# Second-phase shift and scale of both mLSTM layers as dot products on VectorE in the q and k stage, tiles laid out by output channel

## The chip, the cores and the metric

The kernel runs on one core of a Trainium2 chip. The metric is the device time of one execution in microseconds; lower is better. Times of whole executions are given as the median of several runs, and one further execution was recorded by the hardware profiler.

## What is computed

The reference is one inference step of a four-layer trunk for two groups of 128 tokens (context and latent) with width 1024. Layers 0 and 3 mix tokens with an mLSTM, layer 1 with windowed attention, layer 2 with neighbourhood attention. Around every mixer and every ConvFFN stands a norm whose shift, scale and gate are linear in SiLU of a condition vector:

```python
sc = jax.nn.silu(c_ctx)
sl = jax.nn.silu(c)
for i in range(DEPTH):
    mod_c = (sc @ ada_w[i] + ada_b[i]).reshape(6, D_MODEL)
    mod_l = (sl @ ada_w[i] + ada_b[i]).reshape(Bd, 6, 1, D_MODEL)
    hc = _rmsnorm(xc, norm_w[i, 0]) * (1.0 + mod_c[1]) + mod_c[0]
    ...                                   # token mixer: oc, ol
    xc = xc + mod_c[2] * oc
    hc = _rmsnorm(xc, norm_w[i, 1]) * (1.0 + mod_c[4]) + mod_c[3]
    xc = xc + mod_c[5] * _conv_ffn(hc, ...)
```

`ada_w[i]` is 1024 x 6144 in float32. The change concerns `mod[3]` and `mod[4]` (shift and scale ahead of the ConvFFN) of layers 0 and 3: 2048 columns of `ada_w[i]` for each of the two condition vectors.

## The kernel before, in words

All weights come as one stream of tiles, 128 partitions x 2048 float32 (1 MB each), in an order that `stream_order` fixes. SyncE's queue loads them into a ring of four buffers, `raw[0..3]` (L515 to L528). Tile n may be loaded once the tile four places ahead of it in the stream has been released; the loop issues strictly in stream order, so a tile whose buffer is not free also holds back all tiles behind it. 374 tiles go by.

A weight tile is split in two halves of 1024 columns. For each half ScalarE writes a rounded high part (`split_hi`, L460) and VectorE the rest (`split_lo`, L471), into rings of four halves, `spl_hi` and `spl_lo`; TensorE multiplies with both parts. VectorE's `lo_done` releases the raw buffer; TensorE's `half_used` releases the slot of the halves.

An `ada` tile is not split. It has 128 input channels as partitions and 2048 outputs (two of the six vectors) as columns. `ada(i, g)` (L677) multiplies it directly as float32 into the bank `ADA_PS`, in four strips that run beside each other; 8 tiles make a phase, 3 phases a layer, 96 tiles in all. When a phase is complete, `copy_mod` (VectorE, L1676) adds the bias, `mod_rows` (TensorE, L693) transposes, and `mod_columns` (VectorE, L1686) copies into `coef_g` (phase 1, gates) or `coef_b` and `coef_a` (phases 0 and 2, shift and scale; for the scale there follow +1 and the norm's weight). `fill(count)` puts ada tiles between other work; the tables `NORM_FILL`, `CONV_FILL`, `HEAD_FILL`, `V_FILL`, `FFN_FILL` say how many go where.

Each engine's program is written out by hand, in the order in which it runs, with semaphores between engines. An mLSTM layer has these stages:

- ml_x: 8 tiles, convolution, SiLU; then `CONV_FILL` ada tiles and the gates' product.
- q and k: 16 tiles, `ml_qk`, in 8 groups g of two tiles; the first four groups make Q, the last four K. In group g TensorE takes tiles 2g and 2g+1 (`queries_keys`, L569 and L571). VectorE's list for the group is `split_lo` of tile 2g+1, in groups 1 and 2 of Q some small row operations (absolute value, scans, L1845 to L1878), `split_lo` of tile 2g+2, and `with_low` (L1835), which adds the low half of the product to what ScalarE copied out of PSUM. `with_low` must wait until TensorE has finished tile 2g+1. Tile 16 is the first of the v stage.
- scores and transposes (L779, L785), then v: 16 tiles.
- heads: for each of four heads `values`, `state`, `HEAD_FILL` ada tiles, one z tile (`gate_z`, L554 to L556), `head_rows` (L902, transposes of what VectorE normalised in `head`), and another z tile. In layer 0 the gates' `mod_rows` stands behind head 0, in layer 3 in the q and k stage; that of phase 2 stands in head 3 in both.
- down projection, 8 tiles, residual, norm, ConvFFN.

## Time and profile before

| | |
|---|---|
| median of three runs | 1875.69 us (1871.1 to 1875.8) |
| profiled execution, its own time | 1871.99 us |
| span in the profile | 1870.1 us |
| TensorE (PE) busy | 1812.6 us, 97% |
| TensorE weight loads (PEld) | 1501.6 us, 80% |
| VectorE (DVE) busy | 1341.8 us, 72% |
| ScalarE (ACT) busy | 981.0 us, 52% |
| GpSimd (POOL) busy | 178.6 us, 10% |
| DMA | 418.12 MB, mean 224 GB/s |

Busy time is a share of the span. The chain of waits follows the work that ended last back from the last instruction. In rows of the timeline the first number is the start, the second the duration of the row's instructions together, both in us; in brackets stands how long the engine had been idle ahead of it and what released it. "L471" is line 471 of the kernel.

### The profile page before, as it was taken

The numbers are of one execution on the slowest core, as the hardware profiler recorded it, in microseconds if no ns is written. First come the engines' busy times: TensorE is split into PE (matmuls) and PEld (weight loads), VectorE is DVE, ScalarE is ACT, GpSimd is POOL, SyncE is SP. The second block draws the span as 40 slices with busy tenths as digits, with TensorE's granted clock in tenths as the row PEclk, the third lists the DMA queues.
The fourth block names the chain that finished last, engine by engine and source line by source line (L and its number), as shares of the span: only waits on it lengthen the run. The fifth ranks groups of instructions, "written<-read, shape, count | busy, mean of one in ns | idle before, by whom it ended". The sixth has DMA issues, their size and how long they took to land.

```text
span 1870.1 us, 27382 instructions
## 1 busy us (share of the span) xinstructions
PE 1812.6 (97%) x11100; PEld 1501.6 (80%) x11100; DVE 1341.8 (72%) x1973; ACT 981.0 (52%) x1470; POOL 178.6 (10%) x154
## 2 busy tenths in 40 slices
PE   5999999999999999999999999999999999999998
PEld 2988777797888767888877778888888786878888
DVE  3864677668897566998656688966765776769984
ACT  2754445545674354766344466745643445447653
POOL 2100121001000113000011210002100210020001
PEclk8999999999999999999999999999999999999999
DMA  9565556867655757665574766556555647645542
GB/s 365 190 231 195 199 201 229 316 231 275 247 183 198 267 207 292 246 240 189 194 299 172 295 268 267 180 195 242 223 191 184 229 173 286 232 168 195 193 171 84
DMA packets 72527, 418.12 MB, mean 224 GB/s; under 512 B 12176, under 2 KB 18696, under 8 KB 24144
## 3 DMA queue, kind: packets, MB, share of 16 engines
q1 hardware_dynamic: 54288, 392.98, 56.1%
q10 hardware_dynamic: 18112, 23.38, 3.9%
q8 instruction: 88, 1.44, 0.3%
q14 instruction: 39, 0.32, 0.0%
HBM read 405.35 MB, written 10.95 MB: 223 GB/s over the span
## 4 chain that ended last, share of the span: by engine, by line
PE 87%; DVE 5%; DMA 2%; ACT 2%; issue 2%; POOL 1%; POOLq 0%; SPq 0%; DVEq 0%; ACTq 0%
PE ps L587 18%; PE ps L605 9%; PE ps L637 9%; PE ps L589 9%; PE ps L569 6%; PE ps L621 5%; PE ps L638 4%; PE ps L571 3%; PE ps L677 3%; PE ps L554 3%; PE ps L555 3%; PE ps L556 3%; DMA raw<-in_stream 2%; DVE spl_lo L471 2%; PE ps L884 1%
## 5 line engine op out<-in xcount | busy, mean ns | idle before, releaser
L471 DVE TENSOR_TENSOR spl_lo<-raw,spl_hi 128x1024 fp32r<-128x1024 f32 x556 | 686.8, 1258 | 191.3 <-ACT spl_hi L460 191.0
L460 ACT ACTIVATE spl_hi<-raw 128x1024 fp32r<-128x1024 f32 x556 | 574.0, 1053 | 302.6 <-PE ps L638 112.0
L587 PE MATMUL ps<-H,spl_hi 128*128 128x512 f32 x1408 | 496.5, 398 | 4.0 <-DVE H L1750 4.0
L589 PE MATMUL ps<-H,spl_lo 128*128 128x256 f32 x1408 | 393.3, 279 | 0.0
L587 PEld LDWEIGHTS ps<-H,spl_hi 128*128 128x128 f32 x1408 | 264.3, 188 | 79.1 <-issue 15.7
L589 PEld LDWEIGHTS ps<-H,spl_lo 128*128 128x128 f32 x1408 | 265.4, 188 | 0.0
L637 PE MATMUL ps<-G,spl_hi 128*128 128x512 f32 x528 | 184.1, 395 | 0.0
L569 PE MATMUL ps<-B,spl_hi 128*128 128x512 f32 x512 | 179.8, 397 | 0.0
L554 PE MATMUL ps<-H,spl_hi 128*128 128x256 f32 x512 | 148.0, 289 | 6.3 <-DVE H L1750 4.7
L638 PE MATMUL ps<-G,spl_lo 128*128 128x256 f32 x528 | 146.8, 278 | 0.0
L555 PE MATMUL ps<-H,spl_hi 128*128 128x256 f32 x512 | 146.0, 285 | 0.0
L556 PE MATMUL ps<-H,spl_lo 128*128 128x256 f32 x512 | 145.9, 285 | 0.0
L571 PE MATMUL ps<-B,spl_lo 128*128 128x256 f32 x512 | 143.1, 279 | 0.0
L605 PE MATMUL ps<-spl_hi,A 128*128 128x512 f32 x512 | 140.0, 391 | 2.6 <-DVE knat L1888 1.7
L677 PE MATMUL ps<-raw,cond_wide 128*32 128x512 f32 x768 | 103.3, 638 | 20.9 <-DMA raw<-in_stream 11.3
L637 PEld LDWEIGHTS ps<-G,spl_hi 128*128 128x128 f32 x528 | 99.1, 188 | 23.4
L569 PEld LDWEIGHTS ps<-B,spl_hi 128*128 128x128 f32 x512 | 96.1, 188 | 23.3
L605 PEld LDWEIGHTS ps<-spl_hi,A 128*128 128x128 f32 x512 | 95.2, 188 | 23.9 <-ACT v L1187 2.6
L1187 ACT ACTIVATE up<-ps 128x512 f32<-128x512 f32 x88 | 52.6, 598 | 116.3 <-PE ps L589 116.3
L554 PEld LDWEIGHTS ps<-H,spl_hi 128*128 128x128 f32 x512 | 99.2, 194 | 16.1 <-issue 16.0
L555 PEld LDWEIGHTS ps<-H,spl_hi 128*128 128x128 f32 x512 | 99.3, 194 | 0.1
L556 PEld LDWEIGHTS ps<-H,spl_lo 128*128 128x128 f32 x512 | 99.3, 194 | 0.0
(248 smaller groups left out, 2963.4 us busy)
## 6 DMA issues: line engine op xcount, KB each, us to landing
raw<-in_stream SPq DMA_DIRECT2D x374, 1024.0 KB, 4.9
out_new_C<-c_stage ACTq DMA_DIRECT2D x16, 512.0 KB, 3.9
ada_b<-in_ada_b ACTq DMA_DIRECT2D x4, 768.0 KB, 9.9
E<-rows_out ACTq DMA_DIRECT2D x8, 256.0 KB, 4.3
Em<-rows_out ACTq DMA_DIRECT2D x8, 256.0 KB, 4.6
x<-in_x ACTq DMA_DIRECT2D x1, 1024.0 KB, 11.9
wide<-rows_out ACTq DMA_DIRECT2D x8, 128.0 KB, 4.7
cache<-in_na_cache ACTq DMA_DIRECT2D x1, 1024.0 KB, 9.0
```

The lines of the kernel that those rows point to most:

```text
L460: act.activation(spl_hi[m % SPL][:, :], raw[r % RAW][:, h * HALF:(h + 1) * HALF], ACT.Copy).then_inc(S["hi_done"], 1)
L471: dve.tensor_tensor(spl_lo[m % SPL][:, :], raw[r % RAW][:, h * HALF:(h + 1) * HALF], spl_hi[m % SPL][:, :].bitcast(F32), ALU.subtract).the ...
L554: pe.matmul(out, w_hi, x_hi, start=st, stop=False, skip_group_check=True)
L555: pe.matmul(out, w_hi, x_lo, start=False, stop=False, skip_group_check=True)
L556: mm = pe.matmul(out, w_lo, x_hi, start=False, stop=en, skip_group_check=True)
L569: pe.matmul(v3(banks[b][:, :], TOK), w_hi, B_both[:, kk], start=kk == 0, stop=False, skip_group_check=True)
L571: mm = pe.matmul(banks[b][:, 0:TOK], w_lo, B_both[:, kk, 0], start=False, stop=kk == KI - 1, skip_group_check=True)
L587: pe.matmul(banks[:, b * 512:(b + 1) * 512], w_hi, H[:, kk * 512:(kk + 1) * 512], start=kk == 0, stop=False, skip_group_check=True)
L589: mm = pe.matmul(banks[:, b * 512:b * 512 + TOK], w_lo, H[:, kk * 512:kk * 512 + TOK], start=False, stop=kk == KD - 1, skip_group_check=True)
L605: mm = pe.matmul(ACC[2 * s + c][:, :], a, w[m % SPL][:, c * 512:(c + 1) * 512], start=st, stop=en, skip_group_check=True)
L637: pe.matmul(v3(bank[:, :], TOK) if nk == KI else bank[:, :], w_hi, rows(k), start=k == 0, stop=False, skip_group_check=True)
L638: mm = pe.matmul(bank[:, 0:TOK], w_lo, chunk(k)[0], start=False, stop=k == nk - 1, skip_group_check=True)
```

## The change

Of layers 0 and 3 the 8 tiles of phase 2 are no longer `ada` tiles but `ada_column` tiles: same weights, same size, transposed. A tile holds 128 output channels as partitions; its columns 0 to 1023 are the 1024 input channels of the shift, 1024 to 2047 those of the scale. The silu'd condition vectors stand on every partition (`cond_all`, 2048 columns), and each sum over 1024 inputs is one VectorE instruction that multiplies elementwise, writes the products into PSUM (`two[2]`, not read) and the sum into a column of `dots`. Four of them belong to a tile, two in `dot(g, 0)` and two in `dot(g, 1)`; each waits for the one ahead.

The tiles enter the stream in the q and k stage, one in each group, ahead of tiles 2g+2 and 2g+3. `ada` tiles leave the heads (10 and 7 become 2 and 0) and the conv stage of layer 3 (3 becomes 2). The condition vectors are silu'd once at the start as rows, written to DRAM, and read back onto all partitions in each mLSTM layer. `RB` and `RBW` move to a place of their own, since `cond_all` takes theirs. In layer 3 `mod_rows` of the gates moves from the q and k stage to behind head 0. At the end of the heads two additions of the bias and the scale's step make `coef_b` and `coef_a` from `dots`.

```diff
-CONV_FILL = {0: 3, 3: 3}
+CONV_FILL = {0: 3, 3: 2}
 V_FILL = 1
-HEAD_FILL = {0: [2, 3, 3, 2], 3: [2, 2, 2, 1]}
+HEAD_FILL = {0: [2, 0, 0, 0], 3: [0, 0, 0, 0]}
+COLUMN_LAYERS = [0, 3]
...
             order.append(qk[0])
             fill(CONV_FILL[i])
-            order += qk[1:]
+            order.append(qk[1])
+            for g in range(8):
+                order += [("ada_column", i, g)] + qk[2 * g + 2:2 * g + 4]
...
                 if last[0] == "ada":
                     sp.wait_ge(S["ada_used"], INDEX[last] + 1)
+                elif last[0] == "ada_column":
+                    sp.wait_ge(S["dot_done"], 4 * INDEX[last] + 4)
                 else:
                     sp.wait_ge(S["lo_done"], 2 * INDEX[last] + 2)
...
                     queries_keys(n0 + t, 8 * (t % 2), ACC[t // 2 % 2 * 2:t // 2 % 2 * 2 + 2])
-                    if t == 3 and i:
-                        mod_rows(i, 1)
...
-                    if h == 0 and i == 0:
+                    if h == 0:
                         mod_rows(i, 1)
-                    if h + 1 == MH:
-                        mod_rows(i, 2)
...
                     if g == 0:
+                        act.wait_ge(S["condr_kept"], 16)
+                        act.wait_ge(S["xc_lo"], 2 + 8 * (j + 1))
+                        act.wait_ge(S["xcs_done"], 2 + 8 * (j + 1))
+                        act.dma_start(cond_all[:, :], cond_out.rearrange("a b -> (a b)").unsqueeze(0)
+                                      .to_broadcast([P, NS * D])).then_inc(S["conda_landed"], 16)
...
+                act.wait_ge(S["dot_done"], 32 * (j + 1))
                 state_rows(j, 0)
...
+            act.dma_start(cond_row[:, :], io["cond_rows"]).then_inc(S["condr_landed"], 16)
+            act.wait_ge(S["condr_landed"], 16)
+            act.activation(cond_row[:, :], cond_row[:, :], ACT.Silu).then_inc(S["condr_silu"], 1)
+            act.wait_ge(S["condr_silu"], 1)
+            act.dma_start(cond_out, cond_row[:, :]).then_inc(S["condr_kept"], 16)
...
+                def dot(g, n):
+
+                    tile = ("ada_column", i, g)
+                    r = POS[tile]
+                    if n == 0:
+                        landed(dve, r)
+                        if g == 0:
+                            dve.wait_ge(S["conda_landed"], 16 * (j + 1))
+                    for s in range(NS):
+                        o = (n * KD + g) * NS + s
+                        if g + n + s:
+                            dve.wait_ge(S["dot_done"], 32 * j + 4 * g + 2 * n + s)
+                        dve.scalar_tensor_tensor(two[2][:, :], raw[r % RAW][:, n * D:(n + 1) * D], 1.0,
+                                                 cond_all[:, s * D:(s + 1) * D], ALU.mult, ALU.mult,
+                                                 accum_out=dots[:, o:o + 1]).then_inc(S["dot_done"], 1)
...
                     split_lo(dve, n0 + 2 * g + 2)
+                    dot(g, 0)
                     with_low(Q, g, g, DK ** -0.5)
+                    dot(g, 1)
                 for g in range(4):
                     splits(n0 + 8 + 2 * g, 2)
+                    dot(4 + g, 0)
+                    if g == 3:
+                        dot(4 + g, 1)
                     with_low(K, g, 4 + g, 1.0)
+                    if g < 3:
+                        dot(4 + g, 1)
...
-                mod_columns(i, 2)
+                link.wait()
+                dve.wait_ge(S["dot_done"], 32 * (j + 1))
+                for n, coef in enumerate((coef_b, coef_a)):
+                    o = (2 * j + n) * KD
+                    link(dve.tensor_tensor(v3(coef[:, :], NS), v3(dots[:, n * KD * NS:(n + 1) * KD * NS], NS),
+                                           sc("ada_c", o, KD).unsqueeze(2).to_broadcast([P, KD, NS]), ALU.add))
```

## Rows read from the trace of the kernel before

**Rows 1.** The page: busy time by engine, and the chain that ended last.
```profile
PE 1812.6 (97%) x11100; PEld 1501.6 (80%) x11100; DVE 1341.8 (72%) x1973; ACT 981.0 (52%) x1470; POOL 178.6 (10%) x154
...
PE 87%; DVE 5%; DMA 2%; ACT 2%; issue 2%; POOL 1%; POOLq 0%; SPq 0%; DVEq 0%; ACTq 0%
```

**Rows 2.** PE's waits, longest of all: total, times, longest, in us.
```profile
PE ps L677 <- DMA raw<-in_stream: 11.3, 10, 2.4
```

**Rows 3.** Windows: length; busy PE, PEld, DVE, ACT, POOL; clock, DMA share, GB/s.
```profile
38.00:45.00 7.00, 3.75 (x20) 3.50 (x17) 6.79 (x7) 1.64 (x3) 3.88 (x3) 0.68 0.57 209
...
102.00:192.00 90.00, 88.74 (x503) 76.70 (x502) 47.05 (x62) 40.27 (x52) 0.00 (x0) 1.00 0.54 198
301.00:388.00 87.00, 87.00 (x560) 65.00 (x559) 57.53 (x84) 42.77 (x62) 3.54 (x8) 1.00 0.83 309
```

**Rows 4.** Timeline of DVE, one group of the q and k stage, layer 0.
```profile
145.77 0.76 DVE L1835 SCALAR_TENSOR_TENSOR Q<-ps,Q 128x256 f32<-128x256 f32 x2 [3.76 <-ACT Q L1187]
146.99 3.56 DVE L471 TENSOR_TENSOR spl_lo<-raw,spl_hi 128x1024 fp32r<-128x1024 f32 x3 [0.47 <-ACT spl_hi L460]
152.10 1.23 DVE L471 TENSOR_TENSOR spl_lo<-raw,spl_hi 128x1024 fp32r<-128x1024 f32 x1 [1.55 <-ACT spl_hi L460]
157.07 0.76 DVE L1835 SCALAR_TENSOR_TENSOR K<-ps,K 128x256 f32<-128x256 f32 x2 [3.75 <-ACT K L1187]
```

**Rows 5.** Timeline of ACT in the same group.
```profile
148.23 1.06 ACT L460 ACTIVATE spl_hi<-raw 128x1024 fp32r<-128x1024 f32 x1 [0.33 <-PE ps L571]
```

**Rows 6.** Line L528, tiles issued from 100 to 192 us: time to landing.
```profile
DMA to landing us min/median/max: 4.6/4.7/7.3
```

**Rows 7.** Line L528, two tiles issued 0.4 us apart.
```profile
L528 SPq DMA_DIRECT2D raw<-in_stream x2: 328/380/431, 92.6 to 93.0; - x2
...
DMA to landing us min/median/max: 4.8/5.9/7.0
```

**Rows 8.** Timeline of DVE, q and k stage of layer 0.
```profile
111.85 0.75 DVE L1835 SCALAR_TENSOR_TENSOR Q<-ps,Q 128x256 f32<-128x256 f32 x2 [3.76 <-ACT Q L1187]
...
126.65 0.41 DVE L1850 TENSOR_TENSOR gM<-gM,gA 36x256 f32<-36x256 f32 x1
...
130.92 0.41 DVE L1872 SCALAR_TENSOR_TENSOR RB<-gb,gG 36x256 f32<-36x256 f32 x1
131.36 0.32 DVE L1878 TENSOR_SCALAR m_out<-RB 4x1 f32<-4x1 f32 x2
...
190.99 0.75 DVE L1835 SCALAR_TENSOR_TENSOR K<-ps,K 128x256 f32<-128x256 f32 x2 [3.75 <-ACT K L1187]
```

**Rows 9.** The same timeline, layer 3: first and last `with_low`.
```profile
1350.35 0.76 DVE L1835 SCALAR_TENSOR_TENSOR Q<-ps,Q 128x256 f32<-128x256 f32 x2 [3.76 <-ACT Q L1187]
...
1428.66 0.75 DVE L1835 SCALAR_TENSOR_TENSOR K<-ps,K 128x256 f32<-128x256 f32 x2 [3.65 <-ACT K L1187]
```

**Rows 10.** Timeline of ACT, layer 1: exponentials that also sum.
```profile
688.45 0.19 ACT L1475 ACTIVATION_READ_ACCUMULATOR Ea<-ps,nm 128x1 f32 x1
688.54 0.47 ACT L1475 ACTIVATE Ea<-ps,nm 128x256 f32<-128x256 f32 x1
```

**Rows 11.** Timeline of DVE, layer 1: a small operation and one that waits for it.
```profile
687.88 0.16 DVE L2085 SCALAR_TENSOR_TENSOR nm<-mx,nsink 128x4 f32<-128x4 f32 x1
688.08 0.16 DVE L2088 TENSOR_TENSOR esink<-nm,nsink 128x4 f32<-128x4 f32 x1
```

**Rows 12.** Chain of waits: last ada tile ahead of the first norm; heads of layer 0.
```profile
24.80 1.06 PE ps L677 x8
...
324.72 2.71 PE ps L677 x24
...
371.41 1.85 PE ps L677 x16
```

**Rows 13.** Timeline of DVE, layer 3, head 3.
```profile
1611.09 0.69 DVE L1676 TENSOR_TENSOR mod_b<-ps,ada_b 128x512 f32<-128x512 f32 x1
```

**Rows 14.** Timeline of ACT at the start.
```profile
13.10 1.15 ACT L1204 ACTIVATE sq<-x 128x512 f32<-128x512 f32 x2 [3.96 <-DMA x<-in_x]
```

More of the change, by code:

```diff
@@ L83, in stream_order @@
     order = []
-    adas = iter([("ada", i, g) for i in range(DEPTH) for g in range(ADA_TILES)])
+    adas = iter([("ada", i, g) for i in range(DEPTH)
+                 for g in range(2 * ADA_PHASE if i in COLUMN_LAYERS else ADA_TILES)])
     def fill(count):
@@ L150, with mod_index @@
 ADAS = [tile for tile in ORDER if tile[0] == "ada"]
-MAIN = [tile for tile in ORDER if tile[0] != "ada"]
-INDEX = {tile: n for tiles in (MAIN, ADAS) for n, tile in enumerate(tiles)}
+COLUMNS = [tile for tile in ORDER if tile[0] == "ada_column"]
+MAIN = [tile for tile in ORDER if tile[0] not in ("ada", "ada_column")]
+INDEX = {tile: n for tiles in (MAIN, ADAS, COLUMNS) for n, tile in enumerate(tiles)}
+def mod_index(i, phase):
+    return 3 * i + phase - sum(l < i for l in COLUMN_LAYERS)
 def chunked(w, k0, nk, c0, nc):
@@ L191, in host_tile @@
         return np.concatenate([rows[:, v * D:(v + 1) * D] for v in MOD_SOURCE[2 * p:2 * p + 2]], 1)
+    if kind == "ada_column":
+        o = P * tile[2]
+        return np.concatenate([w["ada_w"][i][:, v * D + o:v * D + o + P].T for v in MOD_SOURCE[4:6]], 1)
     if kind == "ml_x":
@@ L266, in host_arrays @@
     put("cond", np.stack([columns(w["c_ctx"]), columns(w["c"][0])], 2).reshape(P, 2 * KD))
+    put("ada_c", np.concatenate([columns(w["ada_b"][i].reshape(6, D)[v]) for i in COLUMN_LAYERS
+                                 for v in MOD_SOURCE[4:6]], 1))
     ada_b = np.zeros((DEPTH, 4, 32, 3, ADA_N), f)
@@ L339, in build @@
     ow = [sb(f"ow{b}", 2 * TOK, F32, rW + 4 * KB + 2 * KB * b) for b in range(2)]
-    RB = sb("RB", 2 * TOK, F32, rW)
-    RBW = sb("RBW", T, F32, rW + 2 * KB)
+    cond_all = sb("cond_all", NS * D, F32, rW)
+    cond_out = nc.dram_tensor("cond_out", (16, P), F32, kind="Internal").ap()
     wide = [sb(f"wide{b}", 2 * T, F32, rW + 4 * KB + KB * b) for b in range(2)]
@@ L388, in build @@
     ccol = small_sb("ccol", NS * 36)
+    RB, RBW = small_sb("RB", 2 * TOK), small_sb("RBW", T)
+    dots = small_sb("dots", 2 * KD * NS)
+    cond_row = small_sb("cond_row", P, rows=16)
     gI, gF, gA, gM, gb, gc, gG = (small_sb(n, TOK) for n in ("gI", "gF", "gA", "gM", "gb", "gc", "gG"))
@@ L672, in ada @@
                 r = POS["ada", i, g]
-                if k == 0 and 3 * i + phase:
-                    pe.wait_ge(S["modT_done"], 3 * i + phase)
+                if k == 0 and i + phase:
+                    pe.wait_ge(S["modT_done"], mod_index(i, phase))
                 landed(pe, r)
@@ L689, in mod_rows @@
             def mod_rows(i, phase):
-                pe.wait_ge(S["modb_done"], 3 * i + phase + 1)
+                pe.wait_ge(S["modb_done"], mod_index(i, phase) + 1)
                 for b in range(4):
@@ L1651, in _ @@
                 if i + 1 < DEPTH:
-                    act.wait_ge(S["modb_done"], 3 * i + 3)
+                    act.wait_ge(S["modb_done"], mod_index(i + 1, 0))
                     act.dma_start(ada_b[:, :], io["ada_b"][i + 1]).then_inc(S["adab_landed"], 16)
@@ L1679, in mod_columns @@
             def mod_columns(i, phase):
-                dve.wait_ge(S["modT_mm"], 3 * i + phase + 1)
+                dve.wait_ge(S["modT_mm"], mod_index(i, phase) + 1)
                 if phase != 1 and link.n:
@@ L1688, in mod_columns @@
                 if phase != 1:
-                    dve.wait_ge(S["modT_done"], 3 * i + phase + 1)
+                    dve.wait_ge(S["modT_done"], mod_index(i, phase) + 1)
                     nw = sc("norm_w", (2 * i + phase // 2) * KD, KD)
@@ L1840, in mlstm @@
                     split_lo(dve, n0 + 2 * g + 1)
-                    if g == 2 and i:
-                        mod_columns(i, 1)
                     if g == 1:
@@ L1931, in mlstm @@
                 split_c(1)
-                if i == 0:
-                    copy_mod(i, 1)
+                copy_mod(i, 1)
                 head_columns(j, 0)
@@ L1939, in mlstm @@
                 z_lo(1)
-                if i == 0:
-                    mod_columns(i, 1)
+                mod_columns(i, 1)
                 for h in range(1, MH):
@@ L1946, in mlstm @@
                     split_z(2 * h + 1)
-                    if h + 1 == MH:
-                        copy_mod(i, 2)
                     head_columns(j, h)
@@ L1959, in mlstm @@
                         split_z(2 * h + 2)
-                mod_columns(i, 2)
+                link.wait()
[4 more added lines that the diff above has]
+                                           sc("ada_c", o, KD).unsqueeze(2).to_broadcast([P, KD, NS]), ALU.add))
+                link.wait()
+                link(dve.scalar_tensor_tensor(v3(coef_a[:, :], NS), v3(coef_a[:, :], NS), 1.0,
+                                              sc("norm_w", (2 * i + 1) * KD, KD).unsqueeze(2).to_broadcast([P, KD, NS]),
+                                              ALU.add, ALU.mult))
                 project(INDEX["ml_down", i, 0], 8, KI, 2 * i)
```

7 lines of the change are left out of this document (3 added, 4 removed).

## The prediction, made before the changed kernel was run

> **What bounds the kernel now.** I read the page first: PE is busy for 97% of the span and holds 87% of the chain that ended last; DVE is busy for 72% [rows 1]. PE's waits come next: the longest in total, ada tiles waiting for their weights, is 11.3 us in the whole span [rows 2]. So the kernel is bound by PE's work, and taking matmuls away should pay if nothing else falls late. The windows say where there is room: in the q and k stage DVE is busy 47 of 90 us, in the heads 57.5 of 87, with PE full in both [rows 3]. By busy shares the change looks good: it moves work from the full engine to a half-empty one. What decides, though, is when the new work stands in DVE's list and when it frees a buffer, so the timeline of one q and k group came next, and the landing times of the tiles behind it.
>
> **One group before.** A group lasts from 145.77 to 157.07, 11.3 us [rows 4]; all of it is PE's two tiles of 5.65 us. DVE adds the low half (0.76), splits three halves (3.56) and, when ACT has it ready, a fourth (1.23), then idles 3.75 us until PE is done. ACT's first high half of a tile takes 1.06 and waits for a slot that PE frees, not for a landing [rows 5]: a tile is asked for four tiles ahead, and lands in 4.7 us [rows 6].
>
> **What is added, step by step.** First one dot. Its operands are 1024 float32, as in `split_lo`; of three of these behind each other two cost (3.56 - 1.23)/2 = 1.17 each [rows 4]. A sum that is written out was seen on ACT only: a read of the accumulator of 0.19 follows the main operation, and the next main one starts 0.09 after the read does [rows 10]. A small DVE operation takes 0.16, and one that waits for it starts 0.20 after its start [rows 11]. The dots wait for each other, so I take 1.17 + 0.20 = 1.37 us from start to start. Bounds: 1.17 if sum and wait are free; 1.5 if the read starts only once the main one has ended and PSUM as a target adds its share. A tile has four: 5.5 us, 44 a layer. The Trainium skill (VectorE: DVE Perf Modes, Two Vector instructions with no wait between them) also counts an operation that writes out its accumulator as two instructions; the trace shows this on ACT alone, and by it the sum would lie near my value and not at the low bound.
>
> By load alone this fits: 0.76 + 4.8 (two tiles' splits) + 5.5 = 11.0 of 11.3 us. But look at the ring. In the stream a group is column tile g, then weight tiles 2g+2 and 2g+3. Four places behind column tile g stands weight tile 2g+4, so SyncE asks for it only when the last of the four dots of g is done, and everything behind it in the stream waits as well. DVE's list from there: end of `dot(g, 1)`; split of tile 2g+3 (2.4 us, in the buffer already); split of tile 2g+4; `dot(g+1, 0)`; `with_low`; `dot(g+1, 1)`. The second split must wait for the landing, and all that is behind it in DVE's list waits too, the dots that free the next buffer among them. So this is a closed cycle:
>
> - landing of a tile: 4.7 median in this stage [rows 6]; a second one is issued right behind it, but of two tiles 0.4 us apart the first landed in 4.8 and only the second in 7.0 [rows 7]. With the semaphore 4.85;
> - high half by ACT, 1.06 [rows 5], and 0.03 until DVE starts: 1.09;
> - two low halves, 1.17 + 1.23 less the overlap: 2.36;
> - two dots, 2.73; `with_low`, 0.76; two dots, 2.73. `with_low` finds PE done: tile 2g+3 starts when its first half is split, 1.2 us into the cycle, and ends at 6.9.
>
> Sum 14.5 us against 11.3, and PE idles for the difference, in two gaps (before 2g+3, its half came late; before 2g+4). Which of the ends of the unknown costs I take hardly matters for the sign: with dots of 1.17 and a landing of 4.6 the cycle is 13.6, still 2.3 above PE's need. It would be PE's again only with dots of 0.55.
>
> The first groups, in layer 0: `with_low` of group 0 starts at 111.85 as before [rows 8]; two dots end at 115.3. Group 1: split of tile 3 until 117.7, row operations 0.6, tile 4 lands at 120.2, its low halves are done at 123.65, dots, `with_low`, dots: 129.9. Group 2: split of tile 5 until 132.25; then the scans, from 126.65 to 131.68 before, 5.05 us [rows 8], which stand ahead of the second split and cover the landing here: 137.3; split 2.36, dots and `with_low` 6.2: 145.9. Groups 3 to 6: 4 x 14.5 = 58. Group 7 has all dots ahead of `with_low`; its end is that of one more cycle: 218.4. Before, the last `with_low` ended at 190.99 + 0.75 = 191.74 [rows 8]. **Layer 0: +26.7 us.** Layer 3 runs the same list; from its first `with_low` to the end of the last it took 1429.41 - 1350.35 = 79.06 before [rows 9] and takes 218.4 - 111.85 = 106.55: **+27.5 us.** The scores and the v stage behind it wait for `with_low` of group 7 and shift whole; the v tiles' buffers are free by then.
>
> **What is removed.** An ada tile in a run costs PE 2.71 / 3 = 0.90 to 1.85 / 2 = 0.93 [rows 12]. Layer 0's heads lose 3, 3 and 2: 7.3 us, and the transposes of phase 2, 0.35. The z tiles that stood behind the fills were split some 2.7 us or more ahead there, so PE takes the whole of it. Layer 3 loses one tile in the conv stage (0.9), 2 in each of heads 0 to 2 and 1 in head 3. There the gates' `mod_rows` now stands behind head 0 and waits for DVE, whose list is not earlier; I count 2.2 for heads 0 and 1 together, 1.85 for head 2 and 1.45 for head 3, where before PE waited for `mod_b` at 1611.09 [rows 13] and now waits for the z tile split just ahead of it. Layer 3: 6.4. **Removed: 14.1 us.** Its bounds: 16 x 0.92 = 14.7 if no cover is missing, 9 if layer 3's heads hang on DVE throughout.
>
> Edits with no price: at the start ACT now waits for `cond_row` to land, behind `x` and `ada_b` in its queue, before the squares, which began at 13.10 [rows 14]. I expect them near 19, done near 24.5; PE adds them up only after the ada tile of 24.80 [rows 12], so 1.4 us of cover is left, and what exceeds it costs as much. `cond_all`, 1 MB, is asked for at about 99 and is first needed at 108; if it lands up to 3 us late, DVE's idle time ahead of 111.85 takes it. The moved `RB`, the bias as columns, the final additions: nothing. GpSimd does nothing in this stage [rows 3].
>
> **Sum.** 1870.1 + 26.7 + 27.5 - 14.1 = 1910.2 us of span, 1912.1 as the profiled execution's own time (1871.99 before, so 1.9 around the span). The median of the runs before is 3.7 above that execution, though its lowest run is 0.9 below it; I add half and say **1914 us**, 2% slower. Bounds: dots of 1.17 or 1.5 give -13 or +8 over two layers, landings of 4.6 give -1, fills -0.6 to +5. If the first tile too suffers from the one issued behind it (7.0 instead of 4.8, in 12 cycles), +26.
>
> **The rivals.**
>
> *The cycle does not close, DVE keeps up* (faster or equal). This needs tile 2g+4 to be there when DVE comes to it. For it: DVE idles 3.75 + 1.55 us in a group, 5.3, nearly the dots' time, and halves are split up to four ahead. Against it: the release hangs on the fourth dot. Only the scans and ACT's extra functions in groups 1 and 2 would then cost, 3 to 6 us a layer. 1870.1 - 14.1 + 9 + 3.7 = 1869 us; it decides if a group of the changed kernel stays below 11.4 us.
>
> *Dots at half rate*: the sum makes each element take twice as long. Another 1.17 for each dot, the pace of 1024 elements [rows 4], is 4.7 in a group; 8 groups and two layers give +75, about 1989 us. DVE alone would then need 15.7 of 11.3 us, so no ring is needed for a loss. Against it stands that a scalar_tensor_tensor on two SBUF sources takes 0.41 on 256 columns, no more than a tensor_tensor [rows 8]; but neither writes a sum. The Trainium skill (Vector Engine (DVE) Microarchitecture Reference, Points that are easy to get wrong) states this rule for two sources that are not bf16: no read port is left for the accumulator. The trace disagrees where there is no sum, and shows no case with one.
>
> *The clock falls.* In the gaps of the cycle PE might be granted 1.2 GHz instead of 2.4, as in the stretch from 38 to 45 us, where the mean was 0.68 after thin work at the start [rows 3]. Each such stretch of 7 us costs at most 3.5 us of PE's work, and as much is idle in a cycle, so even this gives +0 to +20: 1914 to 1934. PE stays 78% busy here; I think it unlikely.
>
> *The change does not do what it says*: tiles or dots elsewhere than in this stage. Nothing in the code speaks for it.
>
> **How the numbers follow.** The closed cycle as summed, 1893 to 1925: 0.70. The cycle with slower landings or a lower clock, up to 1945: 0.11. Half rate, 1970 to 2000: 0.08. DVE keeps up, 1862 to 1875: 0.08, most of it faster by more than 0.3%, which is about what a measurement of this kernel can tell from no change. Small losses between 1875 and 1893: 0.03. The range that holds 8 in 10 is 1893 to 1945; faster 0.06, same 0.03, slower 0.91.
>
> **What would show it.** In the timeline of DVE in the k groups, one `with_low` every 14.5 us; ahead of every second split a wait for ACT's `spl_hi`, and ACT there released by the landing instead of by PE; PE with waits for `spl_lo` of some 3 us a group, about 45 to 50 us in all where now there are next to none; tile 2g+4 issued within 0.1 us of the fourth dot's end; dots of 1.2 with a read of the accumulator behind each of about 0.16. The heads of layer 0 should be 7.7 us shorter. I am wrong if the group stays at 11.3, if the tile is issued ahead of the dots' end, or if a dot takes over 2 us.

## The result, and the profile after

The changed kernel takes 1912.4 us (median of 5 runs, 1909.0 to 1913.9) against 1875.7 for the kernel before (5 runs, 1870.2 to 1876.4). The ratio is 1.0218, with an interval of 1.0200 to 1.0235: 2.2% slower. The forecast was 1914. The profiled execution took 1912.8 us with a span of 1911.0; that of before had 1870.1, so the two traces are compared over +40.9 us.

The page of the changed kernel, busy times and chain, to be held against [rows 1]:

```profile
PE 1820.4 (95%) x10964; PEld 1512.3 (79%) x10964; DVE 1416.4 (74%) x2099; ACT 980.7 (51%) x1471; POOL 178.5 (9%) x154
...
PE 77%; DVE 11%; DMA 5%; ACT 2%; issue 2%; POOL 2%; ACTq 0%; POOLq 0%; SPq 0%; DVEq 0%
```

136 matmuls fewer were recorded, DVE has 75 us more, and it still has a quarter of the span free. What has changed is the chain: PE's part falls from 87% to 77%, DVE's and the landings' part rises from 7% to 16%. PE's waits at two lines stand out (total, times, longest, in us). Before, the first did not show at all, and the second, at L779 there, was 2.5 in total:

```profile
PE ps L590 <- DVE spl_lo L490: 23.3, 18, 2.0
PE ps L798 <- DVE K L1877: 14.3, 2, 7.3
```

L590 is the q and k projection, L798 the scores behind it. Both stand at the stage that received the dots. Windows of that stage (length; busy PE, PEld, DVE, ACT, POOL; clock, DMA share, GB/s) and of the stretch between layer 0's heads and layer 3's q and k stage, to be held against [rows 3]:

```profile
102.00:192.00 90.00, 80.68 (x433) 68.46 (x432) 67.02 (x101) 33.09 (x43) 0.00 (x0) 0.96 0.58 230
...
403.74:1372.83 969.09, 951.01 (x6022) 787.14 (x6021) 729.23 (x1142) 537.37 (x843) 94.33 (x72) 0.99 0.62 232
```

DVE is busy 67 of 90 us where it was 47, PE only 80.7 where it was 88.7. Neither engine is full, which points to a round that goes through both and through something else. DVE's timeline shows it, one group of the k half in layer 0 (start, duration, and in brackets the idle time ahead of the row with its releaser), to be held against [rows 4]:

```profile
170.52 0.75 DVE L1877 SCALAR_TENSOR_TENSOR K<-ps,K 128x256 f32<-128x256 f32 x2
171.19 1.22 DVE L1869 SCALAR_TENSOR_TENSOR ps<-raw,cond_all 128x1024 f32<-128x1024 f32 x1
172.33 0.14 DVE L1869 DVE_READ_ACCUMULATOR ps<-raw,cond_all 128x1 f32 x1
172.50 1.23 DVE L1869 SCALAR_TENSOR_TENSOR ps<-raw,cond_all 128x1024 f32<-128x1024 f32 x1
173.66 0.14 DVE L1869 DVE_READ_ACCUMULATOR ps<-raw,cond_all 128x1 f32 x1
173.66 2.35 DVE L490 TENSOR_TENSOR spl_lo<-raw,spl_hi 128x1024 fp32r<-128x1024 f32 x2
179.75 2.36 DVE L490 TENSOR_TENSOR spl_lo<-raw,spl_hi 128x1024 fp32r<-128x1024 f32 x2 [3.75 <-ACT spl_hi L479]
182.03 1.23 DVE L1869 SCALAR_TENSOR_TENSOR ps<-raw,cond_all 128x1024 f32<-128x1024 f32 x1
...
184.50 0.75 DVE L1877 SCALAR_TENSOR_TENSOR K<-ps,K 128x256 f32<-128x256 f32 x2
```

SyncE's queue and ACT in the same group:

```profile
173.82 2.54 SPq L549 DMA_DIRECT2D raw<-in_stream  x3
...
178.66 2.01 ACT L479 ACTIVATE spl_hi<-raw 128x1024 fp32r<-128x1024 f32 x2 [8.22 <-DMA raw<-in_stream]
```

Read it as one round. The fourth dot's sum is out at 173.80. SyncE issues the next loads at 173.82. DVE splits the two halves of the tile that is already there and then stands still for 3.75 us. ACT, idle for 8.22 us, is released by the landing at 178.66, DVE by ACT at 179.75, and only then come the next dots, which free the next buffer. `with_low` comes at 170.52 and 184.50: 13.98 us for a group, where before it was 11.3 [rows 4]. The idle time of DVE is about the same length as before (3.75), but then it waited for PE at the end of a group, and PE was full; now it waits for memory while PE has run dry.

The first and last `with_low` of both layers, to be held against [rows 8, 9]:

```profile
113.55 0.76 DVE L1877 SCALAR_TENSOR_TENSOR Q<-ps,Q 128x256 f32<-128x256 f32 x2 [1.23 <-ACT Q L1204]
...
215.21 0.42 DVE L1877 SCALAR_TENSOR_TENSOR K<-ps,K 128x256 f32<-128x256 f32 x1
...
1372.83 0.43 DVE L1877 SCALAR_TENSOR_TENSOR Q<-ps,Q 128x256 f32<-128x256 f32 x1 [1.12 <-ACT Q L1204]
...
1474.47 0.75 DVE L1877 SCALAR_TENSOR_TENSOR K<-ps,K 128x256 f32<-128x256 f32 x2
```

From these and the same marks before, the 40.9 us are laid out as follows (us; the stage runs from the first `with_low` to the end of the last; "heads" run from the first product of head 0's `values` to the first of the down projection):

| stretch | before | after | difference | forecast |
|---|---|---|---|---|
| start to first `with_low`, layer 0 | 111.85 | 113.55 | +1.7 | 0 |
| q and k stage, layer 0 | 79.9 | 102.4 | +22.5 | +26.7 |
| scores and v stage, layer 0 | 107.7 | 109.4 | +1.7 | 0 |
| heads, layer 0 | 86.7 | 78.4 | -8.3 | -7.65 |
| to layer 3's first `with_low` | 964.2 | 969.1 | +4.9 | -0.9 |
| q and k stage, layer 3 | 79.1 | 102.4 | +23.3 | +27.5 |
| scores and v stage, layer 3 | 107.7 | 109.5 | +1.8 | 0 |
| heads, layer 3 | 81.0 | 73.7 | -7.3 | -5.5 |
| the rest | | | +0.6 | 0 |
| sum | | | +40.9 | +40.1 |

That the total was met within 2 us is in part luck, because several misses cancel: the stages lost 8.4 us less than forecast, the heads gave 2.5 us more, and some 11 us were lost in places where the forecast has nothing.

### The profile page after: what moved, and what is told of

Its sections match the earlier page's. It is cut to its first block, busy times and chain, and to the rows that moved or that the text cites. A ratio compares the mean times of both kernels' runs of the same rounds, so it can differ in the third digit from the quotient of the medians.

```text
span 1911.0 us, 27255 instructions
## 1 busy us (share of the span) xinstructions
PE 1820.4 (95%) x10964; PEld 1512.3 (79%) x10964; DVE 1416.4 (74%) x2099; ACT 980.7 (51%) x1471; POOL 178.5 (9%) x154
## 4 chain that ended last, share of the span: by engine, by line
PE 77%; DVE 11%; DMA 5%; ACT 2%; issue 2%; POOL 2%; ACTq 0%; POOLq 0%; SPq 0%; DVEq 0%
PE ps L608 17%; PE ps L626 9%; PE ps L658 9%; PE ps L610 9%; DMA raw<-in_stream 5%; PE ps L659 4%; PE ps L642 4%; DVE ps L1869 4%; DVE spl_lo L490 3%; PE ps L575 3%; PE ps L576 3%; PE ps L577 2%; PE ps L698 2%; PE ps L901 1%; PE ps L669 1%
## 5 line engine op out<-in xcount | busy, mean ns | idle before, releaser
L608 PEld LDWEIGHTS ps<-H,spl_hi 128*128 128x128 f32 x1408 | 265.1, 188 | 78.7 <-issue 14.5
L610 PEld LDWEIGHTS ps<-H,spl_lo 128*128 128x128 f32 x1408 | 266.6, 189 | 0.0
L590 PE MATMUL ps<-B,spl_hi 128*128 128x512 f32 x512 | 188.3, 409 | 23.3 <-DVE spl_lo L490 23.3
L590 PEld LDWEIGHTS ps<-B,spl_hi 128*128 128x128 f32 x512 | 99.1, 194 | 52.4 <-DVE spl_lo L490 23.2
L698 PE MATMUL ps<-raw,cond_wide 128*32 128x512 f32 x640 | 90.1, 662 | 18.3 <-ACT cond_wide L1204 9.1
L659 PEld LDWEIGHTS ps<-G,spl_lo 128*128 128x128 f32 x528 | 99.7, 189 | 0.0
```

The costliest lines, as they stand in the source:

```text
L590: pe.matmul(v3(banks[b][:, :], TOK), w_hi, B_both[:, kk], start=kk == 0, stop=False, skip_group_check=True)
L608: pe.matmul(banks[:, b * 512:(b + 1) * 512], w_hi, H[:, kk * 512:(kk + 1) * 512], start=kk == 0, stop=False, skip_group_check=True)
L610: mm = pe.matmul(banks[:, b * 512:b * 512 + TOK], w_lo, H[:, kk * 512:kk * 512 + TOK], start=False, stop=kk == KD - 1, skip_group_check=True)
L659: mm = pe.matmul(bank[:, 0:TOK], w_lo, chunk(k)[0], start=False, stop=k == nk - 1, skip_group_check=True)
```

## The experiments

Two theories stood against each other for the 45.8 us of the q and k stages. *Ring*: the release of a buffer hangs on the fourth dot, and landing, split and dots form a closed round. *Load*: DVE simply has more to do than fits, and every dot costs its time. They part where the work is kept and only the place of the column tile in the stream is changed. The first four kernels ran on one chip beside 9 runs of before (1870.4 us), `e5` and `e6` beside 7 (1870.6), the last two beside 19 (1870.5).

**The column tile one place later.** The work of every engine is as in the changed kernel; weight tile 2g+4 now stands two places behind column tile g, and four behind weight tile 2g+1, which is split early.

```diff
-                order += [("ada_column", i, g)] + qk[2 * g + 2:2 * g + 4]
+                order += qk[2 * g + 2:2 * g + 3] + [("ada_column", i, g)] + qk[2 * g + 3:2 * g + 4]
```

> The same instructions as in the changed kernel; only the column tile moves one place back in the stream, from ahead of tile 2g+2 to between 2g+2 and 2g+3. Its buffer then goes to tile 2g+5 and not to 2g+4, which VectorE needs a whole group later. Ring theory: the waits of 3.7 us ahead of every second split vanish, a group falls from 13.95 to about 11.3 us, and q and k from the first with_low to the end of the last take 80.5 (102.4 less the six waits) to 85 us; the median 1865 to 1876, about 1869. Load theory (VectorE has too much in its list, wherever the tiles come from): the groups stay at 13 to 14 us, over 1900.

Measured: 1878.7 us (1876.1 to 1882.4), ratio 1.0051 [1.0033, 1.0068]. One line of order takes the loss from 2.2% to 0.5%: some 31 us, three quarters of it. In layer 0's stage one wait for a landing is left, 1.2 us of ACT; its length is 88.7 us (113.23 to 201.96) instead of 102.4. The ring is shown, load is refuted as the main cause. But both lie above what I had expected (1865 to 1876 us, a stage of 80.5 to 85): 8.8 us remained in layer 0 and 7.4 in layer 3 (86.5 for 79.1), so part of "load" was right after all. `with_low` of the k groups in DVE's timeline:

```profile
165.79 0.76 DVE L1877 SCALAR_TENSOR_TENSOR K<-ps,K 128x256 f32<-128x256 f32 x2 [1.02 <-ACT K L1204]
...
177.10 0.76 DVE L1877 SCALAR_TENSOR_TENSOR K<-ps,K 128x256 f32<-128x256 f32 x2 [1.02 <-ACT K L1204]
...
188.40 0.76 DVE L1877 SCALAR_TENSOR_TENSOR K<-ps,K 128x256 f32<-128x256 f32 x2 [1.00 <-ACT K L1204]
...
201.21 0.75 DVE L1877 SCALAR_TENSOR_TENSOR K<-ps,K 128x256 f32<-128x256 f32 x2
```

A group takes 11.31, as before, and DVE now waits 1.0 for ACT's copy of PE's product in it instead of 3.75. The last one takes 12.8: there all four dots stand ahead of `with_low`. The rest was lost in groups 1 to 3, the first of it here:

```profile
122.22 2.36 DVE L490 TENSOR_TENSOR spl_lo<-raw,spl_hi 128x1024 fp32r<-128x1024 f32 x2 [2.96 <-ACT spl_hi L479]
...
119.09 0.42 ACT L1302 ACTIVATE gA<-gA 36x256 f32<-36x256 f32 x1 [2.42 <-DVE gA L1885]
119.52 1.28 ACT L1304 ACT_TABLE_LOAD   x1
120.82 0.42 ACT L1304 ACTIVATE gA<-gA 36x256 f32<-36x256 f32 x1
121.14 2.00 ACT L479 ACTIVATE spl_hi<-raw 128x1024 fp32r<-128x1024 f32 x2
```

DVE waits for ACT's high half. ACT had it in its list behind an exponential and a logarithm, and these had waited 2.42 us for a row operation which DVE reached only behind its dots and a split: a round of two engines in each other's way, with no DMA in it. The wait itself is not new: before, DVE waited the same 2.96 us at this place (its split at 118.92) and then another 1.86 ahead of `with_low`. With the dots in its list there is no such slack behind it.

**All four dots ahead of `with_low`**, stream as in the changed kernel.

```diff
                     dot(g, 0)
-                    with_low(Q, g, g, DK ** -0.5)
                     dot(g, 1)
+                    with_low(Q, g, g, DK ** -0.5)
```

(and likewise for k.)

> All four dots ahead of with_low in every group; the instructions and the stream are those of the changed kernel. Ring theory: with_low (0.68) moves into the time of the landing, so a cycle is 13.95 - 0.68 = 13.3 us and some 12 cycles give -8: about 1904. Load theory: nothing changes, 1912. A theory by which with_low, and so TensorE, sets the pace would make it slower.

Measured: 1900.8 us (1899.6 to 1905.4), ratio 1.0168 [1.0147, 1.0188], against 1.0218 for the changed kernel: 0.5%, some 9 us. Two neighbouring groups in DVE's timeline:

```profile
157.46 0.75 DVE L1877 SCALAR_TENSOR_TENSOR Q<-ps,Q 128x256 f32<-128x256 f32 x2
...
163.47 2.36 DVE L490 TENSOR_TENSOR spl_lo<-raw,spl_hi 128x1024 fp32r<-128x1024 f32 x2 [2.99 <-ACT spl_hi L479]
...
170.86 0.75 DVE L1877 SCALAR_TENSOR_TENSOR K<-ps,K 128x256 f32<-128x256 f32 x2
```

The group is 13.40 instead of 13.98: the 0.67 us of `with_low` have left the way from landing to release and lie in the wait (2.99 instead of 3.75). Work on a closed round counts for its full length, the same work beside it for nothing.

**Dots half as wide**, everything else as changed.

```diff
-dve.scalar_tensor_tensor(two[2][:, :], raw[r % RAW][:, n * D:(n + 1) * D], 1.0, cond_all[:, s * D:(s + 1) * D], ...
+dve.scalar_tensor_tensor(two[2][:, 0:512], raw[r % RAW][:, n * D:n * D + 512], 1.0, cond_all[:, s * D:s * D + 512], ...
```

> Each dot goes over 512 of its 1024 columns (the sums are left half done). A dot falls by 0.53 us to 0.79. Ring theory: a cycle of 13.95 - 4 x 0.53 = 11.8 us, still 0.5 above TensorE's need, with a shorter wait for the landing in no group: the waits ahead of the second splits stay at 3.7 us. Load theory: VectorE is far below its limit, groups at 11.3, no such waits. One execution about 1878 (ring) or about 1870 (load).

Measured: 1878.5 us in a single run, so the time alone says little; the trace says more. One round in DVE's timeline:

```profile
169.54 2.36 DVE L490 TENSOR_TENSOR spl_lo<-raw,spl_hi 128x1024 fp32r<-128x1024 f32 x2 [3.67 <-ACT spl_hi L479]
171.82 0.69 DVE L1869 SCALAR_TENSOR_TENSOR ps<-raw,cond_all 128x512 f32<-128x512 f32 x1
172.60 0.70 DVE L1869 SCALAR_TENSOR_TENSOR ps<-raw,cond_all 128x512 f32<-128x512 f32 x1
173.22 0.75 DVE L1877 SCALAR_TENSOR_TENSOR K<-ps,K 128x256 f32<-128x256 f32 x2
...
181.37 2.36 DVE L490 TENSOR_TENSOR spl_lo<-raw,spl_hi 128x1024 fp32r<-128x1024 f32 x2 [3.73 <-ACT spl_hi L479]
```

The round falls to 11.83 (169.54 to 181.37), by 4 x (1.32 - 0.79) = 2.1, and DVE's wait for the landing does not change at all: shorter dots were not used to wait longer, as they would be if another engine set the pace. A round that shrinks by exactly what is taken off it is closed.

**The removal alone.** The kernel before, with the 16 fill tiles of phase 2 taken out of the heads and the conv stage and nothing put in.

```diff
-HEAD_FILL = {0: [2, 3, 3, 2], 3: [2, 2, 2, 1]}
+HEAD_FILL = {0: [2, 0, 0, 0], 3: [0, 0, 0, 0]}
...
-    adas = iter([("ada", i, g) for i in range(DEPTH) for g in range(ADA_TILES)])
+    adas = iter([("ada", i, g) for i in range(DEPTH)
+                 for g in range(2 * ADA_PHASE if i in COLUMN_LAYERS else ADA_TILES)])
```

> The kernel before with the removed part alone: the 16 phase-2 tiles of layers 0 and 3 and what follows from them are left out (the second norms of these layers use the first norms' shift and scale), mod_rows of layer 3's gates stands behind head 0. This prices what the change takes away. By the traces: heads -7.9 and -7.3, conv stage of layer 3 nothing: 1875.7 - 15 = 1861. By the sum of the prediction -14.1: 1861.6. If the fills only covered waits: above 1870.

Measured: 1854.9 us (1853.7 to 1855.5), ratio 0.9916 [0.9896, 0.9935], so 15.5 us below before; the expected 1861 had started from a higher time of before (1875.7). That is what the change had to win if the dots cost nothing. Its first `with_low` stood at 111.83, as before (111.85). From the last `with_low` of layer 0 to the first of layer 3 it takes 1152.6 us, 6.8 less than before; in this stretch the heads of layer 0 lost their eight fill tiles and the conv stage of layer 3 one:

```profile
190.96 0.76 DVE L1835 SCALAR_TENSOR_TENSOR K<-ps,K 128x256 f32<-128x256 f32 x2 [3.74 <-ACT K L1190]
...
1343.55 0.76 DVE L1835 SCALAR_TENSOR_TENSOR Q<-ps,Q 128x256 f32<-128x256 f32 x2 [3.76 <-ACT Q L1190]
```

Not all of the 15.5 us need be the removal's. The two traces differ by 16.4 us, and 3.2 of them lie behind the heads of layer 3 (248.9 us to the end for 252.0), in the last ConvFFN, where no instruction has changed; the kernel with all dots ahead of `with_low` shows 248.9 there too. Up to there the removal won 13.3 us: 7.9 and 7.3 in the heads, less 1.1 in the middle and 0.8 in layer 3's q and k stage.

**Can the win be had?** With up to 15.5 us to win, and 8.8 and 7.4 left in the two stages by the later column tile, DVE's own order was next: dots ahead of `with_low` where it waits, the row operations ahead of the split that ACT's list blocks, and the last group's dots out of the way of its `with_low`. This kernel and the three behind it keep the stream of the first experiment.

```diff
                     dot(g, 0)
-                    with_low(Q, g, g, DK ** -0.5)
                     dot(g, 1)
+                    with_low(Q, g, g, DK ** -0.5)
+                    if g == 0:
+                        (the two row operations gA, gM, moved here from group 1)
...
-                    dot(4 + g, 0)
-                    if g == 3:
-                        dot(4 + g, 1)
+                    if g < 3:
+                        dot(4 + g, 0)
+                        dot(4 + g, 1)
                     with_low(K, g, 4 + g, 1.0)
-                    if g < 3:
-                        dot(4 + g, 1)
+                dot(7, 0)
+                dot(7, 1)
```

> The kernel of e1_one_later with three moves in VectorE's own program. In the groups 0 to 6 both pairs of dots stand ahead of the evacuation with the low parts; in group 7 both stand behind it; and the two row operations that ScalarE's exponential and logarithm wait for stand at the end of group 0 instead of behind the first split of group 1. Theory: what e1_one_later still costs (8.8 us a layer in the q and k stage) is idle time of VectorE that comes from the order of its own program: 2.96 us in group 1 (ScalarE's split parts behind its logarithm), 2.00 in group 3 and 1.02 in each K group ahead of with_low (waiting for ScalarE's copy), and 5.3 of dots ahead of the last with_low. In a K group VectorE's work is 11.31 - 1.02 = 10.3 us, the before kernel's cycle is 10.0. So the stretch from with_low(0) to the last with_low falls from 88.7 to 80.5 to 84 us, K groups come 10.2 to 10.5 us apart, 2 to 5 us of the gain are given back where the dots of group 7 run ahead of the copies of ST: 1862 to 1872 us. Rival: VectorE is simply full in this stage, and each dot costs its time wherever it stands: the stretch stays at 87 to 89 us, the time within 3 us of e1_one_later's 1878.7.

Measured: 1878.1 us (1877.0 to 1881.5), ratio 1.0042 [1.0027, 1.0057]. The stage did what was expected of it: its first and last `with_low` stand at 113.74 and 193.48, 79.7 us apart, against 79.1 before. In layer 0 the dots now cost next to nothing there; in layer 3 the stage still takes 82.3 for 79.1. And the kernel is no faster: 1878.1 is the time that the rival named, though not for its reason, since the stage does not stay at 87 to 89. The place where the gain went is behind the stage (SyncE's queue, ACT's queue, DVE, in that order, then PE's wait):

```profile
199.44 0.80 SPq L549 DMA_DIRECT2D raw<-in_stream  x2
...
204.62 0.33 SPq L549 DMA_DIRECT2D raw<-in_stream  x1
...
199.52 0.41 ACTq L1409 DMA_DIRECT2D E<-rows_out  x1
199.96 0.49 ACTq L1409 DMA_DIRECT2D Em<-rows_out  x1
200.48 0.48 ACTq L1409 DMA_DIRECT2D wide<-rows_out  x1
...
212.76 0.76 DVE L2020 TENSOR_TENSOR E<-E,small 128x256 f32<-128x256 f32 x2 [8.17 <-DMA wide<-rows_out]
...
PE ps L861 <- POOL Pw L2415: 6.5, 2, 4.0
```

The dots of group 7 hold the slot of the last column tile until 199.4. Then two loads of 1 MB, the second kept back only by the first, start 0.4 us apart, at the very moment when ACT asks for the state rows (640 KB in three transfers); a third load follows at 204.62. The last of the rows lands 12.3 us after its issue (12.4 in layer 3); before it took 4.7, with `E` (L1968) at 202.30 instead of 212.76. PE waits at L861 for what hangs on it, and scores and v stage take 115.2 and 113.7 us in the two layers for 107.7 before. (The expectations below speak of three loads at once; the trace shows two.)

**The last group's dots even later**, behind the four copies of `ST` and `knat`:

> As e5_three_moves, and the four dots of group 7 (5.3 us) stand behind the four copies of ST and knat instead of ahead of them. Theory: the copies are what the first splits of the v stage and ScalarE wait for, so ahead of them the dots cost 2 to 5 us in each of two layers, and behind them they lie in the v stage, where VectorE has room: 3 to 9 us below e5_three_moves, 1858 to 1866 us. Rival: the v stage's first split of VectorE is what TensorE waits for at that point, and it comes behind the dots in both kernels: within 2 us of e5_three_moves.

Measured: 1896.2 us (1895.7 to 1896.8), ratio 1.0135 [1.0118, 1.0152]. Both expectations missed, by 30 and by 16 us. The dots end at 207.6; the state rows, which take over the memory of `cond_all`, cannot be asked for before, `E` comes at 221.57 and its rows, again asked for together with two loads, take 12.9 us; PE's wait at L861 is 6.7 at its longest instead of 4.0. I had looked at DVE's list only and not at what waits for the last dot: the ring's slot and `cond_all`'s memory.

**The last group's dots all ahead of `with_low`, and split around it.** Both are `e5_three_moves` with only group 7 changed. Here is the first; in the second `dot(7, 0)` stands ahead of `with_low` and `dot(7, 1)` behind it.

```diff
-                    if g < 3:
-                        dot(4 + g, 0)
-                        dot(4 + g, 1)
+                    dot(4 + g, 0)
+                    dot(4 + g, 1)
                     with_low(K, g, 4 + g, 1.0)
-                dot(7, 0)
-                dot(7, 1)
```

> As e5_three_moves, with the four dots of group 7 ahead of its with_low (ahead of it VectorE stood idle for 3.64 us there, so that 5.3 us of dots put it off by some 1.6). In e5_three_moves the q and k stage already cost what it costs before (79.7 us from with_low(0) to the last one in layer 0), and the kernel was still 7 us slower than before. Theory: those us are lost behind the stage. The four dots of group 7 hold the slot of the last column tile until 199.4; then three transfers of 1 MB start together, within 0.4 us of the state rows' small ones on ScalarE's queue, and these land 12.3 us after their issue where before they took 4.7. With the dots done by 195 the three loads have moved some 2 MB when the rows are issued near 200.7: they land at 206 to 208 instead of 212.8, the stage's end is 1.6 us later, net 2 to 5 us a layer better: 1868 to 1874 us. Rival: the loss has nothing to do with when the dots of group 7 end: then 1.6 us in each of two layers are added, 1880 to 1882 us.

> As e7_all_ahead, with the second pair of group 7 behind the last with_low: with_low is then at 193.5 as in e5_three_moves, and the dots end near 196.8, some 2.5 us before the state rows are issued. Theory (the collision of three 1 MB loads with the state rows): the rows land some 8 to 10 us after their issue, between e5_three_moves (12.3) and e7_all_ahead: 1870 to 1876 us, within 3 us of e7_all_ahead, since the 1.6 us won at with_low are about what the later landing gives back. Rival: the place of the dots against with_low alone decides: 1.6 us a layer below e7_all_ahead.

Measured: all ahead 1871.8 us (10 runs, 1869.4 to 1878.0), ratio 1.0007 [0.9997, 1.0016]; the second pair behind 1875.9 us (10 runs, 1871.2 to 1882.6), ratio 1.0031 [1.0017, 1.0045]. First the kernel with all ahead, then the other: issue of the last state row on ACT's queue, and DVE's first operation on them.

```profile
206.61 0.48 ACTq L1409 DMA_DIRECT2D wide<-rows_out  x1
...
211.25 0.76 DVE L2017 TENSOR_TENSOR E<-E,small 128x256 f32<-128x256 f32 x2 [0.53 <-DMA wide<-rows_out]
```

```profile
200.99 0.49 ACTq L1409 DMA_DIRECT2D wide<-rows_out  x1
...
211.62 0.76 DVE L2019 TENSOR_TENSOR E<-E,small 128x256 f32<-128x256 f32 x2 [6.52 <-DMA wide<-rows_out]
```

With all dots ahead two loads were issued at 198.3, seven to eight us before the state rows, and the last of these lands in 4.6 us; with the last pair behind, they were issued at 197.7 and the rows come 2.3 to 3.3 us after: 10.6. The second kernel had its last `with_low` 3.7 us earlier on the clock (194.43 against 198.16, of which 2.5 come from the start of the kernel) and got nothing for it: `E` starts at the same time. In the first the rows were not asked for near 200.7, as I had expected, but at 205.4 to 206.6, behind the later scores; it is the late issue that kept them clear of the loads.

That the loads stretch the landing of the rows is shown by three kernels that differ only in group 7, in both layers: 12.3 and 12.4 us with the loads at the same moment, 10.6 and 8.8 with the loads shortly ahead, 4.6 and 4.4 with the loads long ahead. What it costs, less what the other order of group 7 gives or takes, is seen between the first and the last of them: in the traces the q and k stages with what follows up to the heads are 8.6 us shorter in the two layers together, and the medians differ by 6.2. The rival, that only the dots' place against `with_low` counts, is refuted: it had the second kernel some 3 us faster, and it is 4.1 slower. But these 4.1 us, more than the 3 that I had allowed, are not explained either. In the traces the same stretches differ by 0.7 us, and the profiled execution of the first kernel (1878.0) was the slowest of its ten.

The time of the first is the same as before within what can be measured. No version was found that is faster than the kernel before. Where the win goes, its trace tells (span 1876.0, so 5.9 above before where the median is 1.3 above): 15.6 us less in the heads, against 7.3 more in the q and k stages (start to start 81.9 for 79.1 in layer 0, 82.9 for 78.3 in layer 3), 4.5 from a later start, 1.6 behind layer 0's stage, and 8.3 in the unchanged middle, which stay open.

## Why the prediction was right, step by step

**The dot, 1.37 forecast, 1.32 measured.** From start to start 171.19 to 172.50 is 1.31; elsewhere 1.32. Multiplying takes 1.22, the read of the accumulator 0.14, and the next starts 0.17 behind the start of the read. The target in PSUM adds nothing that can be seen beside a `tensor_tensor` of the same size (one alone takes 1.23 [rows 4]). The row on ACT [rows 10] gave the right form: a second instruction. The Trainium skill (VectorE: DVE Perf Modes, Two Vector instructions with no wait between them) counts it in the same way, and here the trace agrees on DVE too.

**Half rate, given 0.08: refuted.** A dot of 1024 columns takes 1.23, one of 512 takes 0.69, a `tensor_tensor` of 1024 half of 2.35. The read of the sum takes 0.14 at either width, and nothing is seen that grows with the elements. The Trainium skill's sentence on two sources that are not bf16 (Vector Engine (DVE) Microarchitecture Reference, Points that are easy to get wrong) does not hold for this instruction here; the measurement decides.

**The closed round, 14.5 forecast, 13.98 measured.** Its parts: landing 4.84 (173.82 to 178.66) for 4.85; high half 1.09 for 1.09; two low halves 2.28 (179.75 to 182.03) for 2.36; two dots, `with_low`, two dots 2.47 + 0.67 + 2.64 = 5.78 for 6.22. Most of the half microsecond is the overlap of neighbours: I added durations where I should have added distances from start to start, which [rows 4] gave just as well. Groups 3 to 7 of both layers, ten such rounds, make some 5.5 of the 8.4 us by which the stages came out shorter than forecast; the rest lies in groups 1 and 2 (`with_low` of group 1 was due some 14.5 us after that of group 0 and came 13.93 after it). The fear that the first tile too would land late (+26) did not come true: it landed in the time of a tile that comes alone.

**PE's waits for `spl_lo`, "45 to 50 us": 23.3.** With the wait ahead of the scores, which the forecast did not name, it is 37.6, all of PE's idle time in the two stages, where it was 2.4 before: 35.2 of the 45.8 us. The other 10.6 are PE taking longer over the same matmuls: it is busy for 83.8 and 83.5 us in the two stages, before for 78.7 and 77.9. The third rival, a falling clock, did not set the pace, but the clock did fall; in 10 us windows of the stage the granted clock has dips,

```profile
140.00:150.00 10.00, 8.10 (x41) 6.79 (x40) 8.12 (x13) 2.90 (x4) 0.00 (x0) 0.90 0.29 103
...
170.00:180.00 10.00, 8.01 (x38) 6.69 (x37) 6.22 (x11) 1.78 (x3) 0.00 (x0) 0.83 0.51 197
210.00:220.00 10.00, 3.99 (x20) 3.99 (x21) 6.04 (x12) 0.00 (x0) 0.00 (x0) 0.66 0.43 161
```

where before it was 1.00 throughout [rows 3]. A mean between 0.5 and 1 is a part of the window at the lower of the two levels, 1.2 instead of 2.4 GHz. In the rounds a slower PE only shortens its own wait, since the round is set by the landing and DVE. At the stage's end it is paid, in a place that I had as "shifts whole". There all four dots stand ahead of `with_low`, and PE waits longest of all:

```profile
216.01 5.55 PE L798 MATMUL ps<-Q,K 128*128 128x128 f32 x32 [7.26 <-DVE K L1877]
```

Before, the same 32 matmuls took 3.84:

```profile
191.79 3.84 PE L779 MATMUL ps<-Q,K 128*128 128x128 f32 x32 [1.26 <-DVE K L1835]
```

That is the +1.7 and, in layer 3, +1.8 behind the stage. The other traces bear it out. Wherever PE had waited 1.26 us ahead of the scores (before, the removal alone, and the three kernels that keep a pair of dots or more behind the last `with_low`), they took 3.84 us at a clock of 1.00. Where it had waited 2.8 to 7.3 us, they took 5.5 to 6.8 at a mean clock of 0.54 to 0.69. With all dots ahead and the column tile later PE waited 2.54 us, and both happened: 5.47 us in layer 0, 3.84 in layer 3. Within the five runs of the changed kernel the mean clock was 0.983 to 0.988, within 35 runs of before 0.991 to 0.996.

**The removal, 14.1 forecast, 15.6 by the heads in the table, 13.3 to 15.5 by the run of its own.** Layer 0's heads gave 0.7 us more than forecast. In layer 3 I took 1.8 us too little off, fearing that z tiles would be late behind a missing cover: PE is busy for 73.2 of 73.7 us there. The 0.9 of the conv stage were wrong the other way: 8.17 us for 8.19 before, PE waited for DVE's `A` instead.

**The edits at no price.** The squares began at 18.81 us for "near 19" and the cover of the last ada tile held. Still the first `with_low` came 1.7 us late. PE's row for that tile, to be held against the 1.06 of [rows 12]:

```profile
24.87 1.79 PE L698 MATMUL ps<-raw,cond_wide 128*32 128x512 f32 x8 [1.37 <-DMA raw<-in_stream]
```

The same eight matmuls, started at the same time, took 0.7 us longer. But this is no price of the new work: in the kernel without `cond_row` they took 1.88 us (24.93), and its first `with_low` stood at 111.83. The lateness arises just behind them, in the small matmuls of the first norm, which ran at two speeds. In the changed kernel the eight of `sq` take 1.85 us and the next ada tile starts at 31.58; with the column tile one place later and the three moves, which also computes `cond_row`, they take 1.03 and it starts at 29.68, before at 29.88. First the row of the changed kernel, then that of the other:

```profile
27.47 1.85 PE L736 MATMUL ps<-small,sq 128*128 128x1 f32 x8
...
26.89 1.03 PE L736 MATMUL ps<-small,sq 128*128 128x1 f32 x8
```

Six of the eight kernels with `cond_row` show the slow form and two the fast one, as does the removal alone. So the 1.7 us need not belong to the change; why this stretch runs slow or fast stays open. `cond_all` was asked for at 99.9 and landed in 8.1 to 9.4 us, by 109.3 at the latest, in the cover that I had counted.

**The unchanged middle, +4.9 us with nothing forecast but the 0.9.** Between layer 0's heads and layer 3's first `with_low` PE is busy for 951.0 us where before it was 944.3, for the same matmuls but one ada tile, at a mean clock of 0.99 instead of 1.00. The stretch takes 964.2 us before and 965.4 with the removal alone, and in the eight kernels with the dots 966.6 to 972.5 (966.6 with the column tile one place later). All eight lie above the two without dots, which speaks against mere drift, but each has one trace, and between the last four, whose programs are the same in this stretch, it varies by 4.1 us. What does it was not tried; a forecast has to leave room for it.

## What to carry to other kernels

When work moves into a loop that is fed by a ring of buffers, ask what its last instruction frees and who issues behind it, and add up the round from that release through landing, split and the new work to the next release: if the sum is longer than the loop's pace, busy shares mean nothing, and moving one tile by one place in the stream was worth as much as halving the work that had been added. Inside such a round put ahead of the release only what must be there. A buffer freed late does harm a second time behind the stage, when the loads it held back start together with small, urgent transfers. And when TensorE has had to wait for several us, the matmuls behind the wait may run slower as well.

## What the runs showed of the hardware that was not expected

- Two 1 MB loads issued 0.4 us apart, at the moment of 640 KB in three transfers on another queue, stretched the landing of the last of these from 4.7 to 12.3 us (a third load was issued 4.1 us after it); two loads 2.3 to 3.3 us ahead of them, still to 10.6; 7 to 8 us ahead, 4.6.
- A DVE instruction with an accumulated sum is followed by a read of 0.14 us, whether over 512 or 1024 columns. The instruction itself, with its full output to PSUM, takes 1.22 to 1.23 us over 1024 columns, a `tensor_tensor` to SBUF 1.23. (No dot was run with its output in SBUF.)
- The same load of 1 MB took 8.1 to 9.4 us when it repeated 8 KB from DRAM on 128 partitions, some 4.8 as a tile that comes alone.
- The same 32 matmuls took 3.84 us behind a wait of 1.26 us, and 5.5 to 6.8 us behind waits of 2.8 to 7.3, at a mean granted clock of 0.54 to 0.69.
- The start of a kernel is not a fixed number: in the four last kernels, identical up to there, the first `with_low` stood at 113.74, 115.12, 116.31 and 113.86 us.
